# A block scheme in both halves of a feed-forward output product: four k groups in each, with the sums of one group made earlier

## The reference

```python
h = rms_norm(x, ffn_pre_gain[l])
gt, up = jnp.split(h @ w_ffn_in[l], 2, axis=-1)
x = x + rms_norm((jax.nn.silu(gt) * up) @ w_ffn_out[l], ffn_post_gain[l])
```

## Time and profile before

| | |
|---|---|
| median of the runs | 1490.3 us (1489.94 to 1490.7) |
| profiled execution | 1490.09 us, span 1488.4 us |
| PE busy | 1477.6 us, 99% of the span |
| DVE busy | 1122.2 us, 75% |
| ACT busy | 855.6 us, 57% |
| POOL busy | 151.4 us, 10% |
| HBM traffic | 199 GB/s over the span |

### The profile page before, as it was taken

How to read it: one execution, slowest core, us unless ns; L and a number is a source line. 1 busy time by engine, 2 the same in 40 slices (tenths; PEclk the granted TensorE clock), 3 DMA queues, 4 the chain that set the end, 5 groups by cost and what they waited for, 6 DMA issues and landing times.

```text
span 1488.4 us, 19388 instructions
## 1 busy us (share of the span) xinstructions
PE 1477.6 (99%) x6694; PEld 1216.7 (82%) x6694; DVE 1122.2 (75%) x1317; ACT 855.6 (57%) x1045; POOL 151.4 (10%) x286
## 2 busy tenths in 40 slices
PE   9999999999999999999999999999999999999997
PEld 7888887888888888888888888888888888888876
DVE  6878988855554587657476878988888876887897
ACT  7645455565666544656678556666656654554653
POOL 0000000050220000000000102222220221200000
PEclk9999999999999999999999999999999999999999
DMA  9755555665565655966555576574756656556545
GB/s 341 238 187 177 182 176 190 187 210 186 187 196 171 238 185 178 333 195 212 170 184 184 185 262 211 165 259 159 256 188 213 216 191 242 185 185 224 195 159 198
DMA packets 89859, 305.08 MB, mean 205 GB/s; under 512 B 13056, under 2 KB 13568, under 8 KB 88768
## 3 DMA queue, kind: packets, MB, share of 16 engines
q1 hardware_dynamic: 80144, 285.12, 57.4%
q0 software_dynamic: 9216, 18.63, 3.8%
q10 hardware_dynamic: 432, 0.45, 0.1%
HBM read 294.19 MB, written 2.10 MB: 199 GB/s over the span
## 4 chain that ended last, share of the span: by engine, by line
PE 97%; DVE 2%; DMA 0%; issue 0%; ACT 0%; DVEq 0%; ACTq 0%
PE acc L1894 10%; PE acc L1896 10%; PE acc L1895 10%; PE side L2201 5%; PE side L2200 5%; PE side L2199 5%; PE side L1894 3%; PE side L1896 3%; PE side L1895 3%; PE acc L2201 3%; PE acc L2200 3%; PE acc L2199 3%; PE tr L1896 3%; PE tr L1894 3%; PE tr L1895 3%; PE tr L2199 2%
## 5 line engine op out<-in xcount | busy, mean ns | idle before, releaser
L634 ACT ACTIVATE w_hi<-raw 128x1024 fp32r<-128x1024 f32 x312 | 329.8, 1061 | 266.1 <-PE side L2201 110.9
L1128 DVE TENSOR_TENSOR w_lo<-raw,w_hi 128x1024 fp32r<-128x1024 f32 x324 | 390.9, 1222 | 116.1 <-ACT w_hi L634 105.4
L1123 DVE TENSOR_TENSOR w_lo<-raw,w_hi 128x1024 fp32r<-128x1024 f32 x262 | 320.9, 1227 | 201.5 <-ACT w_hi L616 197.1
L616 ACT ACTIVATE w_hi<-raw 128x1024 fp32r<-128x1024 f32 x262 | 276.9, 1059 | 281.2 <-PE acc L1896 165.7
L1894 PE MATMUL acc<-w_hi,xT_hi 128*128 128x512 f32 x504 | 198.3, 394 | 0.1
L1896 PE MATMUL acc<-w_hi,xT_lo 128*128 128x512 f32 x504 | 196.3, 389 | 0.0
L1895 PE MATMUL acc<-w_lo,xT_hi 128*128 128x512 f32 x504 | 196.3, 389 | 0.0
L589 POOL DMA_DIRECT2D hT_st<-h_blk x176 | 93.5, 540 | 499.1 <-DVE h_blk L1175 470.4
L1894 PEld LDWEIGHTS acc<-w_hi,xT_hi 128*128 128x128 f32 x504 | 94.6, 188 | 22.2 <-issue 2.2
L1896 PEld LDWEIGHTS acc<-w_hi,xT_lo 128*128 128x128 f32 x504 | 94.6, 188 | 20.0
L1895 PEld LDWEIGHTS acc<-w_lo,xT_hi 128*128 128x128 f32 x504 | 94.7, 188 | 19.1
(11 more groups left out here) (482 smaller groups left out, 2870.4 us busy)
## 6 DMA issues: line engine op xcount, KB each, us to landing
raw<-in_units SPq DMA_DIRECT2D x530, 512.0 KB, 4.1
hT_st<-h_blk POOLq DMA_DIRECT2D x176, 32.0 KB, 2.7
x_tok<-in_x SPq DMA_DIRECT2D x4, 512.0 KB, 5.6
qkT<-qk_blk POOLq DMA_DIRECT2D x64, 32.0 KB, 3.2
xres<-in_x POOLq DMA_DIRECT2D x1, 2048.0 KB, 10.7
m_raw<-in_mem_t POOLq DMA_DIRECT2D x1, 2048.0 KB, 8.5
mq<-in_mem POOLq DMA_DIRECT2D x1, 2048.0 KB, 15.3
x_raw<-in_x_t SPq DMA_DIRECT2D x6, 256.0 KB, 6.1
```

Source lines behind the costliest of these rows:

```text
L616: a_.activation(w_hi[:, j % RING], raw[:, j % RING], ACT.Copy).then_inc(hi_ready, 1)
L634: a_.activation(w_hi[:, v % RING], late_raw[slot], ACT.Copy).then_inc(hi_ready, 1)
L1123: v_.tensor_tensor(w_lo[:, s], raw[:, s], w_hi[:, s].bitcast(F32), ALU.subtract).then_inc(lo_ready, 1)
L1128: v_.tensor_tensor(lo[:, v % RING], late_raw[slot], hi[:, v % RING].bitcast(F32), ALU.subtract).then_inc(lo_ready, 1)
```

## The change

Both output halves have four groups, the second in the order 3, 1, 2, 0. The first half begins with eight plain units instead of six, so that products start with the ninth. There are five passes of sums instead of four. Group 0 is summed for each half, and group 3 for both at once. Group 1 is now summed ahead of the first half, into the places of hidden block 10, which makes `hidden_hi(10)` and `hidden_lo(10)` wait for its low part. The pass for group 3 is made in the first half, and the last pass (group 0 again) at the start of the second. In the bodies, `hidden_lo` and `hidden_turn` are issued later. In the first half `hidden_turn(11)` is issued earlier, `hidden_hi(10)` and `hidden_lo(10)` later, and each pass's low part four units ahead of its P5 instead of three.

```diff
--- before.py
+++ after.py
@@ -66,9 +66,9 @@
 EARLY_SLOTS, GROUP_SLOTS = 4, 2 if max(PAIRS) > 1 else 0
 OUT_SLOTS = 3
 SLOTS = RING + EARLY_SLOTS + GROUP_SLOTS + OUT_SLOTS
-OUT_GROUPS = ((0, 1, 2), (0, 1, 2, 3))
-SUMS = (0, 1, 2, 3)
-SUMS_OF = ((1, 2), (3,))
+OUT_GROUPS = ((0, 1, 2, 3), (3, 1, 2, 0))
+SUMS = (0, 1, 2, 3, 0)
+SUMS_OF = ((2, 3), (4,))
 
 
 LEAD = 2
@@ -103,7 +103,7 @@
     plain = [(f"n{n}", UK * g + k) for g in groups[:-2] for n in range(2) for k in range(UK)]
     plain += [(f"n{n}", UK * groups[-2] + k) for n in range(2) for k in range(2 * UK)]
     products = [(kind, g) for g in OUT_GROUPS[m] for kind in ("P1", "P2", "P5", "P7", "P6", "P3", "P4")]
-    return spread(plain, products, len(plain) - 4 - 4 * m, 6 - 2 * m)
+    return spread(plain, products, len(plain) - 4 - 4 * m, 8 - 4 * m)
 
 
 def spread(plain, products, n, lead):
@@ -339,8 +339,8 @@
         S_hi = [at(f"S_hi{g}", kb, [4, 2, P], F32R) for g, kb in enumerate((120, 108))]
         S_lo = [at(f"S_lo{g}", kb, [4, 2, P], F32R) for g, kb in enumerate((164, 152))]
         e_sb = at("e_sb", 200, [NC])
-        h_f = [at(f"h_f{k}", kb, [4, SEQ]) for k, kb in enumerate((164, 48, 48, 60, 60)[:len(SUMS)])]
-        H_f = [at(f"H_f{k}", kb, [4, 2, P]) for k, kb in enumerate((120, 52, 52, 52, 52)[:len(SUMS)])]
+        h_f = [at(f"h_f{k}", kb, [4, SEQ]) for k, kb in enumerate((164, 160, 48, 48, 60)[:len(SUMS)])]
+        H_f = [at(f"H_f{k}", kb, [4, 2, P]) for k, kb in enumerate((120, 116, 52, 52, 52)[:len(SUMS)])]
         H_hi = [at(f"H_hi{k}", kb, [4, 2, P], F32R) for k, kb in enumerate((72, 168, 176))]
         H_lo = [at(f"H_lo{k}", kb, [4, 2, P], F32R) for k, kb in enumerate((76, 172, 196))]
         H_hi, H_lo = H_hi + H_hi[:1], H_lo + H_lo[:1]
@@ -1070,7 +1070,9 @@
                 if k == 2:
                     act.wait_ge(hT_ready, 11)
                 if k == 3:
-                    act.wait_ge(unit_used, OUTS[1].first + OUTS[1].order.index(("P4", 0)) + 1)
+                    act.wait_ge(unit_used, OUTS[0].first + OUTS[0].order.index(("P4", 0)) + 1)
+                if k == 4:
+                    act.wait_ge(unit_used, OUTS[1].first + OUTS[1].order.index(("P4", 3)) + 1)
                 act.wait_ge(hs_ready, k + 1)
                 a_.activation(H_hi[SUMS[k]][:].rearrange("p m q t -> p (m q t)"), H_f[k][:].rearrange("p m q t -> p (m q t)"),
                               ACT.Copy).then_inc(hs_hi, 1)
@@ -1080,7 +1082,10 @@
                 for v in range(b.first, b.end):
                     if v == S_FO + 1:
                         sums_hi(0)
-                    if v == S_FO + 2:
+                    if v == S_FO + 4:
+                        sums_hi(1)
+                    if v == S_FO + 8:
+                        act.wait_ge(hs_lo, 2)
                         hidden_hi(10)
                     if v == S_FO + 16:
                         hidden_hi(11)
@@ -1763,12 +1768,12 @@
                         dve.wait_ge(s_lo, 1)
                         x_sums(1)
                     if i > 1 and v == b.first:
-                        if i > 2:
-                            hidden_lo(i - 2)
                         hidden_product(i - 2)
+                    if i > 2 and v == b.first + 3:
+                        hidden_lo(i - 2)
                     if i == 2 and v == b.first + 1:
                         x_sums_lo(1)
-                    if i > 1 and v == b.first + (5 if i == 2 else 1):
+                    if i > 1 and v == b.first + 6:
                         hidden_turn(i - 1)
                     if b.p and v == b.last["P6"]:
                         dve.wait_ge(unit_used, v + 1)
@@ -1803,6 +1808,8 @@
                     hidden_turn(10)
                 if v == BODIES[9].end + 6:
                     hidden_sums(0)
+                if v == BODIES[9].end + 9:
+                    hidden_sums(1)
                 split_late(v + RING)
 
             def y3_part_of(n, h):
@@ -1823,22 +1830,28 @@
 
             for m, b in enumerate(OUTS):
                 n0 = 2 * m
-                sums_at = {b.first + b.order.index(("P5", SUMS[k])) - 8: k for k in SUMS_OF[m]}
+                sums_at = {b.first + b.order.index(("P5", SUMS[k])) - 8: k for k in SUMS_OF[m] if m == 0}
+                los_at = {b.first + b.order.index(("P5", SUMS[k])) - 4: k for k in SUMS_OF[m]}
                 for v in range(b.first, b.end):
+                    if m == 1 and v == b.first + 10:
+                        hidden_sums(4)
                     if v == S_FO:
                         hidden_product(10)
-                    if v == S_FO + 3:
+                    if v == S_FO + 2:
+                        dve.wait_ge(hT_turned, 10 * 256)
+                        hidden_turn(11)
+                    if v == S_FO + 4:
                         hidden_sums_lo(0)
-                    if v == S_FO + 4:
+                    if v == S_FO + 6:
+                        hidden_sums_lo(1)
+                    if v == S_FO + 10:
                         hidden_lo(10)
-                    if v == S_FO + 6:
-                        hidden_turn(11)
                     if v == S_FO + 20:
                         hidden_lo(11)
                     if v in sums_at:
                         hidden_sums(sums_at[v])
-                    if v - 5 in sums_at:
-                        hidden_sums_lo(sums_at[v - 5])
+                    if v in los_at:
+                        hidden_sums_lo(los_at[v])
                     if v == b.last["P6"] + 1:
                         dve.wait_ge(unit_used, b.last["P6"] + 1)
                         sum_p6(m + 1, y3_part_of(n0, 0), y3_part_of(n0 + 1, 0))
@@ -2278,7 +2291,7 @@
                             pe.wait_ge(u_done, 1)
                         late_product(v, side[:, 2], *h_block(g, 0, 0), begin)
                     if kind == "P5":
-                        pe.wait_ge(hs_lo, g + 1)
+                        pe.wait_ge(hs_lo, 5 if (m, g) == (1, 0) else g + 1)
                         late_product(v, side[:, 3], *sum_of(H_hi[g], H_lo[g], 0), begin)
                     if kind == "P6":
                         late_product(v, tr[:, 1], *sum_of(H_hi[g], H_lo[g], 1), begin)
```

## The result

The changed kernel takes 1498.4 us (median of five runs, 1497.7 to 1499.3) against 1490.3 us; the ratio is 1.0053, with a 95% interval of 1.0042 to 1.0065. The forecast was slower, with 1494.9 us; the measured time is 0.5 us above the stated range. The profiled execution of the changed kernel took 1497.7 us (span 1495.8), 7.4 us of span more than that of before.

What follows compares the result with a forecast made beforehand. TensorE was taken to bound the kernel (busy 99% of the span, 97% of the chain). The terms -1.36 + 0 + 2.7 + 4.4 - 1.1 = +4.6 us, added to 1490.3, gave 1494.9 us, range 1492.6 to 1497.9.

Steps and rivals of the forecast that it cites:

- 1. The matmuls: First output half: a fourth group replaces four plain units by seven products, six matmuls fewer, -1.36 us of PE.
- 2. What was moved without cost: Second pass of sums ahead of the first half, later low parts and transposes in the bodies: 0, bounds 0 to 1 us.
- 3. The wait on the spread: First half, position 20: last spread landed at 1292.1, PE waits for w_lo, +2.7 us, bounds +0.4 and +4.2.
- rival D: Short landing: the spread's DMAs take an estimated 2.1 us each, sum +2.7, 1493.0 us; chance 0.10.
- 4. DVE in the dense stretch: First half from the ninth unit: DVE falls behind, waits +1.8, +1.2 and +1.3, together +4.4 us, bounds 0 and +5.5.
- The second sign of being wrong: The prediction is wrong if DVE shows idle time before w_lo between 1296 and 1346 us.
- 5. The second half: Pass of sums moved to position 10: the 1.3 us stall falls to about 0.2, -1.1 us, bounds -1.3 and 0.
- A: DVE keeps up in the first half, only the spread's wait is left: +0.2, 1490.5 us; chance 0.10.
- B: Everything is covered, the spread too: -2.7, 1487.6 us; chance 0.05.
- C: Spread interrupted: one or two gaps of 1.48 us in its issues, +6.1 to +7.6, 1496.4 to 1497.9 us; chance 0.15.

Runs made afterwards that it cites:

- e2_pass2_early_lead6: e7_pass2_early with products from the seventh unit of the first half (six plain units first instead of eight); 1488.4 us, ratio 0.9985 to the kernel before.
- e3_bodies_back: Changed kernel with the bodies' old order: hidden_lo at the first unit, hidden_turn at the second (sixth in body 2); 1498.8 us, ratio 1.0055 to before.
- e8_before_take_10: Kernel before with hidden_hi(11) at unit 10 of the first half instead of 16; 1495.4 us (one run).
- e1_late_take: Changed kernel with hidden_hi(11) at unit 20 of the first half (was 16) and hidden_lo(11) at 24 (was 20); 1492.4 us, ratio 1.0013 to before.
- e5_hold_loads: Changed kernel where SyncE holds the weight loads that split S_FO + 17 and later would free until the last spread has landed; 1494.5 us (one run).
- e7_pass2_early: e1_late_take with the pass of sums for group 2 at unit 3 of the first half instead of eight units ahead of its P5; 1490.3 us, ratio 0.9998.
- e9_late_lead6: e1_late_take with products from the seventh unit of the first half instead of the ninth, group 2's pass of sums not moved; 1490.7 us, ratio 1.0003.
- e10_last_low_early: Kernel before with the second half's group 3 pass of sums at its unit 10 and low part four units ahead of P5, not three; 1489.6 us, ratio 0.9995.

## Why the prediction was right and wrong

**1. The matmuls: right.** 1008 of them at 0.2267 us, six fewer; the first half of e2_pass2_early_lead6 takes 114.31 us.

**2. What was moved without cost: right.** PE has no new wait in the bodies, and e3_bodies_back is no faster. The one new wait before 1249 us (0.5 us, 12.8 us after the start) lies in code that the change doesn't touch; e8_before_take_10, which has the same code there, shows one of 0.7 us at that place.

**3. The wait on the spread: the mechanism right, the size wrong, and this is the step that failed.** ACT's activation waited at the place named, the product of the second group waited for it, and e1_late_take takes 6 us out with it. The forecast was 2.7 us; the wait took 4.8, and the slow matmuls 1.7 more behind it. Two things were wrong. First, the landing of the last DMAs: I took the 4.0 us of the trace of before and bounded it from above by a gap in the issues. I did not ask what else would be under way at the new time. It was 6.3 us, and e5_hold_loads, by bringing it down to 2.5, shows that the loads beside it are the cause. The spread landed 2.4 us later than forecast, hence 2.1 us more of wait. The 2.1 us that the prediction estimated from the Trainium skill's page "DMA: Bandwidth & Descriptors" (section "Anatomy of one DMA — SWDGE (gpsimd) path", my rival D) is near what such a DMA took with few loads beside it (1.7 at the least, a median of 2.5 for the last four with the loads held), and not near 6.3. Second, the clock: I priced a wait of PE at its own length. A wait of 2.7 us would have lain between the two points measured since, 2.0 and 3.05 us, and the text should have named the fall to half pace as a bound of +1.7. The first half of the earlier trace rows said that the clock stood at the upper level, but not what a wait does to it.

**4. DVE in the dense stretch: 4.4 forecast, 3.2 measured.** The waits at the P7 of the third and fourth group were forecast as 1.2 and 1.3 us and came as 1.1 and 1.5, at the tr<- products named. The rest of the 3.2 is steps too wide by up to 0.24 us. The 1.8 us of the second group didn't come: DVE resumed 1.3 us ahead of PE, as forecast, and the slow matmuls then gave it 1.7 us. Without them the waits appear (1.5 us in pieces in e5_hold_loads, 0.9 us in e1_late_take, where the activation stands elsewhere). So terms 3 and 4 were not independent. What the clock added to one it took from the other, and the cancelling was luck. By the traces, 2.1 of the 2.8 us that the forecast of the difference was short are the landing. The second sign of being wrong did not show: from 1297 to 1346 us DVE was never idle before a w_lo. e7_pass2_early and e9_late_lead6 confirm the cause, the pass of sums and the density.

**5. The second half: right.** The stall of 1.3 us (1.1 by the starts of the matmuls) is down to 0.1, as in e10_last_low_early. That both the pass and its low part are needed I had put as one.

**The rivals.** A (covered by DVE) and B (all covered) did not happen, but e2_pass2_early_lead6 realises nearly what B counted: 2.7 us at most, 2.1 measured. C named the size (6.1 to 7.6 us) with another mechanism: there was no gap in the issues. The sum of terms 1, 2, 4 and 5 was wrong by 1.1 us, term 3 by 3.8 the other way. The range held C's 7.6 us but not the lower clock on top of anything. The 7.4 us of the traces, added to 1490.3, would have lain inside it, on C's account and not on the forecast's.

## What to carry to other kernels

When a step is moved, ask three things of what hangs on it: what it releases (here 16 DMAs, through a buffer freed later), who takes that and at which place in his own order, and what else uses the same DMA engines at the new time. A wait of the bounding engine may cost more than its length, so price it with the clock behind it, and then ask which later waits the slower stretch takes away. And where a second engine is 90% busy in a stretch, place its long steps (a pass of sums of 2.85 us) where it still waits for others: the same work cost 2 us in one place and nothing in the other.

## What the runs showed of the hardware

The last small DMAs of a spread of GpSimd's (32 KB, inside SBUF) landed 2.5, 4.0 or 6.3 us after their issue: with no 512 KB load of SyncE issued in the 2.8 us before them (e5_hold_loads), with three such loads issued among the 8.5 us of the spread's issues (before), and with five in under 4 us of them (changed). Their issue took 0.54 us each in all three cases. The Trainium skill's page "DMA: Bandwidth & Descriptors" (section "Queues, rings and completion order") says that each DMA engine takes packets from its queues in turn. By that a small transfer on a queue of its own still shares the engine with the loads; the landings agree.

The granted clock fell to 0.54 for 3.7 us after waits of 3.05 and 4.66 us and stayed at 1.00 after 2.00 us. Where it turns between these was not tried. The waits of 3.05 and 2.00 us are one execution each.
